# FFN down projections as seven block products per K pair instead of eight, in four passes, with POOL forming the differences of weight blocks

## The chip, the cores and the metric

One NeuronCore of a Trainium2 chip runs the whole program. The metric is the device time in microseconds (us) of one execution; the median of three timed executions of the kernel before is 2356.09 us. Engines: PE is TensorE's matmul stream and PEld its weight loads, DVE is VectorE, ACT is ScalarE, POOL is GpSimd, SP is SyncE, which issues the loads here.

## What is computed

Two decoder layers on a residual stream of 512 tokens by 1024 features, all float32. Each layer has two SwiGLU feed-forward blocks (FFN), a token mixer and a cross-attention. Only the FFN is touched by the change, and in it the last product:

```
def swiglu(x, w_gate, w_up, w_down):
    return (jax.nn.silu(x @ w_gate) * (x @ w_up)) @ w_down

h += 0.5 * rms_norm_post(swiglu(rms_norm_pre(h), w_gate, w_up, w_down))   # four times in all
```

w_gate and w_up are 1024 x 2816, w_down is 2816 x 1024. The 2816 hidden features are 22 blocks of 128, taken two at a time: 11 pairs ("groups" in gate_up, "quads" in the changed down stage).

## The kernel before, in words

**Split operands.** Every large product is made of three matmuls: each operand is written as hi + lo, both of type fp32r, and `three` (lines 1680 to 1684) issues hi x lo, lo x hi and hi x hi into the same PSUM bank. A matmul here has 128 x 128 stationary and 512 moving columns (256 in a few places).

**Pieces of weights.** Weights come as pieces of 128 x 1024 float32. SP loads a piece into one of four slots of `raw` (`load`, L428). ACT writes its hi part to `whi` (`split`, L642 with a gain for gate_up, L638 without one), DVE subtracts and writes the lo part to `wlo` (L1074, L1069), and PE uses both. `whi` and `wlo` have four slots too. Splits run three pieces ahead of PE (LOOKAHEAD = 3): ACT may overwrite a slot when `pieces_used` says that PE is done with the piece four before, and SP may reload a raw slot when `lo_made` says that its lo part exists. Each engine takes its instructions strictly in the order in which the program was written, so a split, an eviction and a sum that stand in DVE's queue are done in that order whatever is ready.

**Stages.** A list of stages (`stages`) sets the order. An FFN before is gate_up of 6 groups, down, gate_up of 5 groups, down. A gate_up group is 4 pieces of 24 matmuls (256 gate and 256 up columns, features in the partitions). Behind it DVE scales the two results out of PSUM into `gate` and `up` (L1385, L1388), ACT applies Silu (L869), POOL multiplies (L592), ACT writes `mid_hi` (L871) and DVE `mid_lo` (L1391), two blocks of 128 features by 512 tokens. A down stage has two groups, one for each half of 512 output columns; a piece is two K blocks by 512 columns, and `token_major` runs for each K block and each of four token tiles the three matmuls, so a K block costs 24 matmuls in all. A group uses four PSUM banks, the next one the other four; DVE releases them after reading (`release_banks`).

**Result.** The first pass of an FFN is copied to `y_rows` (L1456), the second is added (L1133). `close_sublayer` then takes squares for the norm (ACT L669, `square_result`), the variance (DVE L1137), a power on POOL (`power`, L543), the gain (DVE L1144) and the update of `h` (DVE L1179, `update`). `last_group` on PE orders the last group by token tile and puts transposes of updated tiles of `h` (`updated_units`, L1764) among its matmuls, so that the next stage can open: `open_hi` (ACT L654) and `open_lo` (DVE L1102) make `xhi` and `xlo` from them, and `first_group` starts with half of the tokens.

POOL also makes constant tables once, in the first down stage (`make_tables`, L531 to L577), which even_in uses.

Of the kernel before, what the change touches and what calls it, by code (L numbers as in the profile page):

```python
# [35 lines left out]
D = 1024  # L36
SEQ = 512
MEM = 256
FF = 2816
# [18 lines left out]
FF_PASSES = ((0, 6), (6, 5))  # L58
# [7 lines left out]

def stages():
# [3 lines left out]
    def ffn(l, j):  # L71
        for n, (g0, ng) in enumerate(FF_PASSES):
            out.append(("gate_up", l, (j, n), ng, KT // PK))
            out.append(("down", l, (j, n), 2, ng))
# [26 lines left out]
def build(nc, A, out):  # L101
# [65 lines left out]
    rows = place("rows", [P, 3, P], f32, at(3072))  # L167
    lam_in = place("lam_in", [P, 4, 64], f32, at(3456))
# [6 lines left out]
    mid_hi = place("mid_hi", [P, 12, SEQ], f32r, at(0))  # L175
    mid_lo = place("mid_lo", [P, 12, SEQ], f32r, at(6144))
    gate = place("gate", [P, 2, SEQ], f32, at(12288))
    up = place("up", [P, 2, SEQ], f32, at(13312))
# [47 lines left out]
    def sem(name):  # L226
# [25 lines left out]
    gate_scaled, up_scaled, gate_silu, product_ready, mid_hi_ready, mid_lo_ready = map(sem, (  # L252
        "gate_scaled", "up_scaled", "gate_silu", "product_ready", "mid_hi_ready", "mid_lo_ready"))
# [50 lines left out]
    def straight_groups(ng):  # L304

        return 2 if ng % 2 == 0 else 1

# [11 lines left out]
    def ends_sublayer(kind, arg):  # L319
        return kind in ("mix_out", "xo") or (kind == "down" and arg[1] == 1)  # L320
# [18 lines left out]
    def columns(g):  # L339
        return slice(g * GC, (g + 1) * GC)  # L340

# [60 lines left out]
    def _(sp):  # L402
# [18 lines left out]
        def load(base, g, halves):  # L421


            slot = base % RAW_SLOTS
            if not isinstance(base, int) or base >= RAW_SLOTS or not isinstance(g, int) or g:
                sp.wait_ge(lo_made, base + 1 + 4 * g)
            for dst, src in halves(slot):
                sp.dma_start(dst, src).then_inc(raw_full[slot], 16)  # L428

# [33 lines left out]
        piece = ended = 0  # L463
        for kind, l, arg, ng, np_ in STAGES:
            first_piece = piece
            if kind == "gate_up":
                j, n = arg
                first = straight_groups(ng)
                g0 = FF_PASSES[n][0]
                for g in range(first):  # L470
                    for kp in range(4):
                        if piece + 4 * g + kp == 0:
                            load_x(0)
                        if piece + 4 * g + kp == 1:
                            load_x(1)
                        if piece + 4 * g + kp == RAW_SLOTS:
                            load_rest()
                        load(piece + 4 * g + kp, 0, gate_and_up(l, j, kp, (g0 + g) * 256))
                with sp.Fori(0, (ng - first) // 2) as i:
                    for q in range(2):  # L480
                        for kp in range(4):
                            load(piece + 4 * (first + q) + kp, 2 * i,
                                 gate_and_up(l, j, kp, (g0 + first + q) * 256 + i * 512))
                piece += 4 * ng
                continue
            for g in range(ng):
                for n_piece in range(group_pieces(kind, g, np_, arg)):
# [4 lines left out]
                    elif kind == "down":  # L492
                        j, n = arg
                        src = two_rows(A["ffn_w_down"][l, j], 2 * FF_PASSES[n][0] + 2 * kp, g * GC)
# [12 lines left out]
                    load(piece, 0, src)  # L507
# [18 lines left out]
    def _(pool):  # L526
# [52 lines left out]
        products = 0  # L579
        for kind, l, arg, ng, np_ in STAGES:  # L580
# [6 lines left out]
            if kind == "gate_up":  # L587
                def multiply(n):

                    pool.wait_ge(gate_silu, n)  # L590
                    pool.wait_ge(up_scaled, n)
                    g.tensor_tensor(up[:], gate[:], up[:], MUL).then_inc(product_ready, 1)  # L592
                first = straight_groups(ng)
                for q in range(first):
                    multiply(products + q + 1)
                with pool.Fori(0, (ng - first) // 2) as i:
                    for q in range(2):
                        multiply(products + first + q + 1 + 2 * i)
                products += ng
            elif kind == "down" and (l, arg) == (0, (0, 0)):  # L600
                make_tables()
            elif kind == "even_in":
# [24 lines left out]
    def _(act):  # L627
# [3 lines left out]
        def split(n):  # L631

            slot = n % RAW_SLOTS
            act.wait_ge(raw_full[slot], 32 * (n // RAW_SLOTS + 1))
            act.wait_ge(pieces_used, n + 1)
            gains = piece_gain[n]
            if gains is None:
                a(flat(whi[:, slot]), flat(raw[:, slot]), ACT.Copy).then_inc(hi_made, 1)  # L638
                return
            hi, full = piece_rows(whi, slot, len(gains)), piece_rows(raw, slot, len(gains))  # L640
            for k, c in enumerate(gains):
                last = a(hi[:, k, :], full[:, k, :], ACT.Copy, scale=vec[:, c:c + 1])  # L642
            last.then_inc(hi_made, 1)
# [16 lines left out]
        def square_result(kind, bank, t, g):  # L660

            src = PS[:, bank + t, :]
            if kind == "down":
                E.await_(y_ready)
                src = y_rows[:, t, columns(g)]
# [6 lines left out]
        def square_tile(kind, bank, t, done):  # L672
# [3 lines left out]
            elif kind != "down":  # L676
                E.await_(tile_done)
            square_result(kind, bank, t, 1)

        def close_sublayer(kind, n, n_stage):  # L680
# [4 lines left out]
            if kind != "down":  # L685
                act.wait_ge(pieces_used, done)
# [5 lines left out]
            if kind == "down":  # L692
                E.seen[tile_done.name] += TT - 1

            def next_h(t):
# [1597 lines left out]
```

## Time and profile before

| | |
|---|---|
| three timed runs | 2354.50, 2356.09, 2356.28 us; median 2356.09 us |
| the profiled execution | 2354.63 us, of which the span from first to last instruction is 2352.9 us |
| granted clock of TensorE, mean | 0.997 of full |
| PE busy | 2331.8 us, 99% of the span, 12035 matmuls |
| PEld busy | 1976.7 us, 84% |
| DVE busy | 1151.1 us, 49%, 1531 instructions |
| ACT busy | 881.6 us, 37%, 1442 instructions |
| POOL busy | 179.0 us, 8%, 150 instructions |
| DMA | 217.48 MB, mean 92 GB/s |

Busy time counts the time in which at least one instruction of the engine is in flight. Matmuls overlap: each is shown for 0.39 us, but a new one starts more often than that, so what a matmul costs in a dense stretch is read from starts and not from durations. Timeline rows give the start in us from the start of the span, then the duration, then engine, line and operation; in square brackets stands how long the engine sat idle before, and what ended that.

### The profile page before, as it was taken

The numbers are of one execution on the slowest core, as the hardware profiler recorded it, in microseconds if no ns is written. First come the engines' busy times: TensorE is split into PE (matmuls) and PEld (weight loads), VectorE is DVE, ScalarE is ACT, GpSimd is POOL, SyncE is SP. The second block draws the span as 40 slices with busy tenths as digits, with TensorE's granted clock in tenths as the row PEclk, the third lists the DMA queues.
The fourth block names the chain that finished last, engine by engine and source line by source line (L and its number), as shares of the span: only waits on it lengthen the run. The fifth ranks groups of instructions, "written<-read, shape, count | busy, mean of one in ns | idle before, by whom it ended". The sixth has DMA issues, their size and how long they took to land.

```text
span 2352.9 us, 30267 instructions
## 1 busy us (share of the span) xinstructions
PE 2331.8 (99%) x12035; PEld 1976.7 (84%) x12035; DVE 1151.1 (49%) x1531; ACT 881.6 (37%) x1442; POOL 179.0 (8%) x150
## 2 busy tenths in 40 slices
PE   8999999999999999999999999999999999999998
PEld 7888888888888888888888888888878888888887
DVE  4433436595645444433454433455996544443434
ACT  4322324444444443323333322335265443322322
POOL 0131100000000001100101000000000000100000
PEclk9999999999999999999999999999999999999999
DMA  5233332311222123233223332322322212332231
GB/s 183 81 108 98 92 114 76 104 63 58 79 83 97 63 72 111 86 107 99 94 95 99 98 99 90 107 90 90 108 72 84 88 54 90 99 108 94 85 107 72
DMA packets 170483, 217.48 MB, mean 92 GB/s; under 512 B 12952, under 2 KB 120824, under 8 KB 170360
## 3 DMA queue, kind: packets, MB, share of 16 engines
q1 hardware_dynamic: 170248, 215.75, 28.8%
q8 instruction: 84, 1.38, 0.2%
q14 instruction: 39, 0.32, 0.0%
q10 hardware_dynamic: 112, 0.03, 0.0%
HBM read 213.63 MB, written 2.10 MB: 92 GB/s over the span
## 4 chain that ended last, share of the span: by engine, by line
PE 98%; DVE 1%; ACT 1%; issue 0%; DMA 0%; ACTq 0%; POOLq 0%; POOL 0%; DVEq 0%
PE ps L1682 29%; PE ps L1683 29%; PE ps L1684 29%; PE ps L2120 1%; PE ps L2233 1%; PE ps L1764 1%; PE ps L2050 1%; PE ps L1866 1%; PE ps L2158 1%; PE ps L2064 0%; PE ps L1734 0%; PE ps L2209 0%; PE ps L2147 0%; PE ps L1718 0%; PE ps L2160 0%
## 5 line engine op out<-in xcount | busy, mean ns | idle before, releaser
L1682 PE MATMUL ps<-xlo,whi 128*128 128x512 f32 (+1 forms) x2032 | 752.1, 370 | 1.7 <-DVE wlo L1074 1.7
L1683 PE MATMUL ps<-xhi,wlo 128*128 128x512 f32 (+1 forms) x2032 | 748.9, 369 | 0.0
L1684 PE MATMUL ps<-xhi,whi 128*128 128x512 f32 (+1 forms) x2032 | 748.8, 368 | 0.0
L1074 DVE SCALAR_TENSOR_TENSOR wlo<-raw,vec,whi 128x512 fp32r<-128x512 f32 (+1 forms) x488 | 338.6, 741 | 412.4 <-ACT whi L642 411.1
L642 ACT ACTIVATE whi<-raw,vec 128x512 fp32r<-128x512 f32 (+1 forms) x488 | 318.6, 708 | 486.2 <-PE ps L1684 450.9
L1682 PEld LDWEIGHTS ps<-xlo,whi 128*128 128x128 f32 x2032 | 384.0, 189 | 65.7 <-issue 2.1
L1684 PEld LDWEIGHTS ps<-xhi,whi 128*128 128x128 f32 x2032 | 383.7, 189 | 63.9
L1683 PEld LDWEIGHTS ps<-xhi,wlo 128*128 128x128 f32 x2032 | 383.9, 189 | 63.1
L1069 DVE TENSOR_TENSOR wlo<-raw,whi 128x1024 fp32r<-128x1024 f32 x152 | 185.5, 1227 | 286.2 <-ACT whi L638 284.7
L638 ACT ACTIVATE whi<-raw 128x1024 fp32r<-128x1024 f32 x152 | 159.4, 1056 | 336.3 <-PE ps L1684 335.8
L1682 PE MATMUL ps<-wlo,mid_hi 128*128 128x512 f32 x704 | 274.4, 390 | 0.0
L1684 PE MATMUL ps<-whi,mid_hi 128*128 128x512 f32 x704 | 274.0, 389 | 0.0
L1683 PE MATMUL ps<-whi,mid_lo 128*128 128x512 f32 x704 | 273.9, 389 | 0.0
L592 POOL TENSOR_TENSOR up<-gate,up 128x1024 f32<-128x1024 f32 x44 | 105.2, 2391 | 1069.7 <-DVE up L1388 1069.7
L1684 PEld LDWEIGHTS ps<-whi,mid_hi 128*128 128x128 f32 x704 | 132.2, 188 | 27.5
L1683 PEld LDWEIGHTS ps<-whi,mid_lo 128*128 128x128 f32 x704 | 132.2, 188 | 27.2
L1682 PEld LDWEIGHTS ps<-wlo,mid_hi 128*128 128x128 f32 x704 | 132.2, 188 | 27.1
L1682 PE MATMUL ps<-wlo,xhi 128*128 128x512 f32 x352 | 138.7, 394 | 2.5 <-issue 2.5
L1684 PE MATMUL ps<-whi,xhi 128*128 128x512 f32 x352 | 137.2, 390 | 0.0
L1683 PE MATMUL ps<-whi,xlo 128*128 128x512 f32 x352 | 137.0, 389 | 0.0
L1391 DVE TENSOR_TENSOR mid_lo<-up,mid_hi 128x1024 fp32r<-128x1024 f32 x44 | 54.8, 1244 | 161.5 <-ACT mid_hi L871 161.5
L869 ACT ACTIVATE gate<-gate 128x1024 f32<-128x1024 f32 x44 | 46.7, 1061 | 223.6 <-DVE gate L1385 223.6
(248 smaller groups left out, 2213.4 us busy)
## 6 DMA issues: line engine op xcount, KB each, us to landing
raw<-ffn_w_gate_dram SPq DMA_DIRECT2D x176, 256.0 KB, 2.8
raw<-ffn_w_up_dram SPq DMA_DIRECT2D x176, 256.0 KB, 3.0
raw<-ffn_w_down_dram SPq DMA_DIRECT2D x176, 256.0 KB, 3.1
raw<-xattn_w_kv_dram SPq DMA_DIRECT2D x64, 256.0 KB, 3.0
raw<-even_w_in_dram SPq DMA_DIRECT2D x56, 256.0 KB, 2.9
raw<-odd_w_in_dram SPq DMA_DIRECT2D x42, 256.0 KB, 2.8
raw<-xattn_w_q_dram SPq DMA_DIRECT2D x32, 256.0 KB, 3.0
raw<-xattn_w_o_dram SPq DMA_DIRECT2D x32, 256.0 KB, 3.0
```

The lines of the kernel that those rows point to most:

```text
L592: g.tensor_tensor(up[:], gate[:], up[:], MUL).then_inc(product_ready, 1)
L638: a(flat(whi[:, slot]), flat(raw[:, slot]), ACT.Copy).then_inc(hi_made, 1)
L642: last = a(hi[:, k, :], full[:, k, :], ACT.Copy, scale=vec[:, c:c + 1])
L869: a(gate[:], gate[:], ACT.Silu).then_inc(gate_silu, 1)
L1069: v.tensor_tensor(flat(wlo[:, slot]), flat(raw[:, slot]), flat(whi[:, slot]).bitcast(f32), SUB).then_inc(lo_made, 1)
L1074: last = v.scalar_tensor_tensor(out=lo[:, k, :], in0=full[:, k, :], scalar=vec[:, c:c + 1], in1=hi[:, k, :].bitcast(f32), op0=MUL, op1=SUB)
L1391: v.tensor_tensor(mid_lo[:, 2 * g:2 * g + 2, :], up[:], mid_hi[:, 2 * g:2 * g + 2, :].bitcast(f32), SUB).then_inc(mid_lo_ready, 1)
L1682: mm(out_ap, lh, rl, start=start, stop=False, skip_group_check=skip_group_check)
L1683: mm(out_ap, ll, rh, start=False, stop=False, skip_group_check=skip_group_check)
L1684: return mm(out_ap, lh, rh, start=False, stop=stop, skip_group_check=skip_group_check)
L1764: last = T(x_unit(bank, t, b)[:, k, :], h[:, t, (4 * b + k) * P:(4 * b + k + 1) * P], ident[:])
L1866: last = nc.tensor.transpose(blocks_of(4, 6)[:, n, :], probs[:, i % 2, m, kt * P:(kt + 1) * P], ident[:])
```

## The change

The 22 K blocks of w_down are paired. For one pair ("quad" q) the tokens are cut into two halves of 256, the output columns into two halves of 512, and the 2 x 2 by 2 x 2 block product is formed with seven products: A11 B11 (P1), A12 B21 (P2), S4 B22 (P3), A22 T4 (P4), S1 T1 (P5), S2 T2 (P6), S3 T3 (P7). A are blocks of the hidden activations and S sums of them, B are blocks of the weight and T differences: T1 = B12 - B11, T2 = B22 - T1, T3 = T2 - B11, T4 = B21 - T2. A product of one quad is two token tiles of three 128x512 matmuls.

* **Passes.** An FFN has four passes with gate_up groups 3, 2, 3, 3 and down quads 2, 3, 3, 3. A down stage has one list of units (one unit is one 128x512 block of B or T), two to a piece: first the units of B21, B11 and T1 of all quads but the last, then those of the last quad, then T2, B22, T3, T4.
* **PE.** `down` runs P2, P1, P5 of the early quads, then of the last one, then P6, P3, P7, P4, token tile by token tile. P1 and P6 and P7 and P4 share two banks: P6 accumulates on P1 after DVE has read P1, and so on, so PE waits for `product_read` before P6, P3, P7 and for each tile of P4.
* **DVE.** Before: one read per tile and group of columns in two passes (32 copies, 32 adds). After: in each pass P1, P2, P5, P6 are read two tiles at a time (128x1024) and P3, P7, P4 tile by tile. The reads stand in the queue between the splits. `gate` and `up` become halves of one tile `mid`; the wait ahead of the gate eviction is for the whole chain of the group before. Four sums of 128x256 (S1 to S4) follow POOL's product. `mid_lo` is made in two instructions (three and four blocks of 256 tokens), with splits between them in the last group of a stage.
* **ACT.** Splits of units (128x512); `mid_hi` in two instructions, likewise with splits between them.
* **POOL.** T1 ahead of the last product of a gate_up stage. In the down stage: T2 as one instruction per raw slot (128x1024, and 128x512 where there are three quads), then T3 and T4 (each 128 x 512 nq elements). `make_tables` moves to even_in.
* **SP.** B11, B12 and B21 are loaded to tiles of their own (`load_corners`, 3 nq loads of 256 KB) behind the first gate_up group's loads; B22 goes through the raw slots. The hardware loops over gate_up groups are written out.

The core of the diff (PE's and DVE's placement, POOL's work):

```diff
-FF_PASSES = ((0, 6), (6, 5))
+FF_GROUPS = ((0, 3), (3, 2), (5, 3), (8, 3))
+FF_QUADS = ((0, 2), (2, 3), (5, 3), (8, 3))
+def down_units(nq):
+    early, late = range(nq - 1), nq - 1
+    out = [("B21", q) for q in early] + [("B11", q) for q in early] + [("T1", q) for q in early]
+    out += [("B11", late), ("B21", late), ("T1", late)]
+    return out + [(name, q) for name in ("T2", "B22", "T3", "T4") for q in range(nq)]
```

POOL, in gate_up:

```diff
+                for g_ in range(ng):
+                    if g_ == ng - 1:
+                        pool.wait_ge(w11_loaded, 16 * (quads + nq))
+                        pool.wait_ge(w12_loaded, 16 * (quads + nq))
+                        difference(k, w12, flat(w12[:, 0:nq, :]), flat(w11[:, 0:nq, :]))
+                    products += 1
+                    pool.wait_ge(gate_silu, products)
+                    pool.wait_ge(up_scaled, products)
+                    g.tensor_tensor(mid[:, 4:8, :], mid[:, 4:8, :], mid[:, 0:4, :], MUL).then_inc(product_ready, 1)
```

POOL, in a down stage:

```diff
+                pool.wait_ge(lo_made, t1_piece + 1 + RAW_SLOTS)
+                for i in range(0, nq, 2):
+                    n = min(2, nq - i)
+                    ins = g.tensor_tensor(w12[:, i:i + n, :], raw[:, (first_raw + i // 2) % RAW_SLOTS, 0:n, :],
+                                          w12[:, i:i + n, :], SUB)
...
+                E.own()
+                pool.wait_ge(combined, 4 * k + 2)
+                difference(k, w11, flat(w12[:, 0:nq, :]), flat(w11[:, 0:nq, :]))
+                pool.wait_ge(w21_loaded, 16 * (quads + nq))
+                difference(k, w21, flat(w21[:, 0:nq, :]), flat(w12[:, 0:nq, :]))
```

ACT, in gate_up:

```diff
                     act.wait_ge(gate_scaled, mids)
-                    a(gate[:], gate[:], ACT.Silu).then_inc(gate_silu, 1)
+                    a(mid[:, 4:8, :], mid[:, 4:8, :], ACT.Silu).then_inc(gate_silu, 1)
+                    if g == ng - 1:
+                        split_next()
                     act.wait_ge(product_ready, mids)
-                    a(mid_hi[:, 2 * g:2 * g + 2, :], up[:], ACT.Copy).then_inc(mid_hi_ready, 1)
+                    a(mid_hi[:, slot, 4:7, :], mid[:, 4:7, :], ACT.Copy).then_inc(mid_hi_ready, 1)
+                    if g == ng - 1:
+                        split_next()
+                    act.wait_ge(sums_ready, mids)
+                    a(mid_hi[:, slot, 0:4, :], mid[:, 0:4, :], ACT.Copy).then_inc(mid_hi_ready, 1)
```

DVE, in gate_up behind the evictions of gate and up:

```diff
+                    if g == ng - 1:
+                        split_next()
+                    dve.wait_ge(product_ready, mids)
+                    a12, a22, a11, a21 = [mid[:, 4 + n, :] for n in range(4)]
+                    E.run(v.tensor_tensor(mid[:, S1, :], a21, a22, ADD))
...
+                    dve.wait_ge(mid_hi_ready, 2 * mids - 1)
+                    v.tensor_tensor(mid_lo[:, slot, 4:7, :], ...).then_inc(mid_lo_ready, 1)
+                    if g == ng - 1:
+                        split_next()
+                    dve.wait_ge(mid_hi_ready, 2 * mids)
+                    v.tensor_tensor(mid_lo[:, slot, 0:4, :], ...).then_inc(mid_lo_ready, 1)
```

DVE, in a down stage:

```diff
+            at_piece = {2: ("P1", "P2", "P5"), 3: ("P6",), 4: ("P3a", "P3b"), 5: ("P7a", "P7b"), 6: ("P4a", "P4b")} if nq == 2 else \
+                {3: ("P1", "P2"), 4: ("P5",), 6: ("P6",), 7: ("P3a", "P3b"), 8: ("P7a",), 9: ("P7b",), 10: ("P4a", "P4b")}
+            for n in range(2, len(down_pieces(nq))):
+                split_next()
+                for name in at_piece.get(n, ()):
+                    read[name]()
```

DVE, in the last pass of an FFN (`close_down`):

```diff
+            open_lo(0, x_banks[0])
+            split_next()
+            read["P4a"]()
+            made = weigh(2, 0)
+            open_lo(1, x_banks[1])
+            split_next()
+            read["P4b"]()
```

PE, in a down stage behind P1, P2 and P5:

```diff
+            pe.wait_ge(product_read, r0 + 1)
+            for t in range(2):
+                one_tile(u0, t, S2, x)
+            pe.wait_ge(product_read, r0 + 3)
+            for t in range(2):
+                one_tile(u0 + nq, t, S4, z)
+            pe.wait_ge(product_read, r0 + 4)
+            for t in range(2):
+                one_tile(u0 + 2 * nq, t, S3, x)
+            E.group += 2
+            if opens:
+                wait_banks(E.group)
+                updated_units(0)
+            pe.wait_ge(product_read, r0 + 7)
+            one_tile(u0 + 3 * nq, 0, A22, x, range(1))
+            if opens:
+                updated_units(1)
+            one_tile(u0 + 3 * nq, 0, A22, x, range(1, nq))
+            pe.wait_ge(product_read, r0 + 8)
+            one_tile(u0 + 3 * nq, 1, A22, x)
```

## Rows read from the trace of the kernel before

**Rows 1.** The page: span, busy time, and the chain that ended last.
```profile
span 2352.9 us, 30267 instructions
...
PE 2331.8 (99%) x12035; PEld 1976.7 (84%) x12035; DVE 1151.1 (49%) x1531; ACT 881.6 (37%) x1442; POOL 179.0 (8%) x150
...
PE 98%; DVE 1%; ACT 1%; issue 0%; DMA 0%; ACTq 0%; POOLq 0%; POOL 0%; DVEq 0%
```
**Rows 2.** Groups by form on PE: count, busy us, mean ns of one.
```profile
L1682 PE MATMUL ps<-wlo,mid_hi 128*128 128x512 f32 x704 | 274.4, 390 | 0.0
```
**Rows 3.** Timeline of DVE: the same instruction behind two successive gate_up groups.
```profile
281.71 1.22 DVE L1385 TENSOR_TENSOR gate<-ps,rsb 128x1024 f32<-128x1024 f32 x1 [2.59 <-PE ps L1684]
...
303.47 1.22 DVE L1385 TENSOR_TENSOR gate<-ps,rsb 128x1024 f32<-128x1024 f32 x1 [2.59 <-PE ps L1684]
```
**Rows 4.** Timelines around the start of the first down stage.
```profile
150.95 0.39 PE L1682 MATMUL ps<-wlo,mid_hi 128*128 128x512 f32 x1
...
151.15 1.23 DVE L1385 TENSOR_TENSOR gate<-ps,rsb 128x1024 f32<-128x1024 f32 x1 [3.06 <-PE ps L1684]
...
153.65 2.39 POOL L592 TENSOR_TENSOR up<-gate,up 128x1024 f32<-128x1024 f32 x1 [19.37 <-DVE up L1388]
...
156.08 1.06 ACT L871 ACTIVATE mid_hi<-up 128x1024 fp32r<-128x1024 f32 x1 [2.60 <-POOL up L592]
```
**Rows 5.** Groups by form on DVE, ACT and POOL: count, busy us, mean ns.
```profile
L1095 DVE TENSOR_TENSOR xlo<-y,xhi 128x512 fp32r<-128x512 f32 x28 | 18.4, 688 | 18.2 <-ACT xhi L734 18.2
...
L734 ACT ACTIVATE xhi<-y 128x512 fp32r<-128x512 f32 x28 | 16.5, 623 | 12.5 <-DVE y L1611 12.3
...
L592 POOL TENSOR_TENSOR up<-gate,up 128x1024 f32<-128x1024 f32 x44 | 105.2, 2391 | 1069.7 <-DVE up L1388 1069.7
```
**Rows 6.** Timeline of DVE: four successive 128x512 instructions.
```profile
352.43 2.48 DVE L1133 TENSOR_TENSOR y_rows<-ps,y_rows 128x512 f32<-128x512 f32 x4 [3.06 <-PE ps L1684]
```
**Rows 7.** Timeline: POOL and DVE at once, in the first down stage.
```profile
157.08 1.09 POOL L533 TENSOR_SCALAR_AFFINE_SELECT head_sel_f<-head_sel_f 8x1024 f32<-8x1024 f32 x1
157.17 2.07 DVE L1391 TENSOR_TENSOR mid_lo<-up,mid_hi 128x1024 fp32r<-128x1024 f32 x1 [3.66 <-ACT mid_hi L871]
...
168.62 1.23 DVE L1069 TENSOR_TENSOR wlo<-raw,whi 128x1024 fp32r<-128x1024 f32 x1 [4.13 <-ACT whi L638]
168.69 1.30 POOL L575 CAST level_mask<-level_f 128x128 int8<-128x128 f32 x1
...
171.79 0.29 POOL L575 CAST level_mask<-level_f 128x128 int8<-128x128 f32 x1
```
**Rows 8.** Single lines of code: duration ns min/median/max, first and last start.
```profile
L616 POOL TENSOR_TENSOR ring<-ring,conv x2: 1277/1744/2212, 1783.1 to 1786.3; 128x512 f32<-128x512 f32 x2
L616 POOL TENSOR_TENSOR ring<-conv x1: 1441/1441/1441, 1723.3 to 1723.3; 128x512 f32<-128x512 f32 x1
...
L1326 DVE TENSOR_SCALAR conv<-u,vec x4: 540/542/1495, 1646.4 to 1723.5; 128x512 f32<-128x512 f32 x4
```
**Rows 9.** Timeline of PE: 256-column matmuls at the start of the kernel.
```profile
12.42 0.55 PE L1682 MATMUL ps<-xlo,whi 128*128 128x256 f32 x1 [1.74 <-DVE wlo L1074]
...
16.19 0.41 PE L1684 MATMUL ps<-xhi,whi 128*128 128x256 f32 x1
16.40 0.31 PE L1682 MATMUL ps<-xlo,whi 128*128 128x256 f32 x1
...
16.67 0.28 PE L1684 MATMUL ps<-xhi,whi 128*128 128x256 f32 x1
16.79 0.28 PE L1682 MATMUL ps<-xlo,whi 128*128 128x256 f32 x1
```
**Rows 10.** One stretch: busy us (instructions) by engine, granted clock, DMA.
```profile
590.00:592.00 2.00, 2.00 (x10) 2.00 (x11) 0.14 (x2) 0.66 (x1) 0.00 (x0) 0.50 0.00 0
```
**Rows 11.** Timelines around the end of the first FFN: last results of tiles 2, 3.
```profile
383.79 0.93 POOL L543 TENSOR_TENSOR rstd<-var,neg_half 128x1 f32<-128x1 f32 x1 [1.95 <-DVE var L1137]
...
385.56 1.28 DVE L1179 SCALAR_TENSOR_TENSOR h<-y_rows,rstd,h 128x1024 f32<-128x1024 f32 x1
```

More of the change, by code:

```diff
@@ L64, with down_pieces, piece_of @@
 N_VEC = CONV_TAPS + CONV_W * CONV_T
+def down_units(nq):
[3 more added lines that the diff above has]
+    return out + [(name, q) for name in ("T2", "B22", "T3", "T4") for q in range(nq)]
+def down_pieces(nq):
+    units = down_units(nq)
+    corners, sums = units[:3 * nq], units[3 * nq:]
+    return [part[n:n + 2] for part in (corners, sums) for n in range(0, len(part), 2)]
+def piece_of(nq, unit):
+    return unit // 2 if unit < 3 * nq else (3 * nq + 1) // 2 + (unit - 3 * nq) // 2
 def stages():
@@ L461, in forget_rows @@
             return halves
-        piece = ended = 0
+        piece = ended = loads = 0
         for kind, l, arg, ng, np_ in STAGES:
@@ L506, in _ @@
                         src = two_rows(w, 2 * kp, g * GC)
-                    load(piece, 0, src)
+                    load(loads, src)
+                    loads += 1
                     piece += 1
@@ L579, in _, with difference @@
         products = 0
+        def difference(k, out, a_, b_):
+            nq = downs[k][3]
+            E.run(g.tensor_tensor(flat(out[:, 0:nq, :]), a_, b_, SUB), combined)
         for kind, l, arg, ng, np_ in STAGES:
@@ L691, in close_sublayer @@
             E.group += 2
-            if kind == "down":
-                E.seen[tile_done.name] += TT - 1
-            def next_h(t):
-                E.await_(h_ready)
-                act.wait_ge(h_squared, E.made[h_squared.name])
-                square_h(t, h_scratch[:])
-            if not opens(n_stage):
-                for t in range(TT):
-                    square_tile(kind, second, t, done + n)
-                return
             square_tile(kind, second, 0, done + n)
@@ new lines, in close_down, with gained, weigh, release @@
+        def close_down(k, n_stage):
+            read = reads_of(k, False)
+            def gained(t, g):
+                quarter = y_rows[:, t, columns(g)]
+                E.run(v.tensor_tensor(quarter, quarter, post_gain[:, columns(g)], MUL),
+                      post_gain_used if (t, g) == (TT - 1, 0) else None)
+                return E.last
+            def weigh(t, g):
+                result_variance("down", t)
+                return gained(t, g)
+            def release():
+                E.release_banks()
+                E.group += 1
+            split_next()
+            split_next()
+            read["P1"]()
+            read["P2"]()
+            split_next()
+            read["P5"]()
+            split_next()
+            read["P6"]()
+            dve.wait_ge(post_gain_loaded, 16 * (ended[0] + 1))
+            ended[0] += 1
+            for t in range(2):
+                E.await_(y_squared)
+                gained(t, 0)
+            split_next()
+            read["P3a"]()
+            made = weigh(0, 1)
+            read["P3b"]()
+            release()
+            split_next()
+            update(0, made)
+            read["P7a"]()
+            made = weigh(1, 1)
+            update(1, made)
+            read["P7b"]()
+            for t in (2, 3):
+                E.await_(y_squared)
+                gained(t, 1)
+            if not opens(n_stage):
+                read["P4a"]()
+                made = weigh(2, 0)
+                update(2, made)
+                read["P4b"]()
+                release()
+                made = weigh(3, 0)
+                update(3, made, 2)
+                return
+            x_banks = [x_bank(t, E.group + 1) for t in range(TT)]
+            open_lo(0, x_banks[0])
+            split_next()
+            read["P4a"]()
+            made = weigh(2, 0)
+            open_lo(1, x_banks[1])
+            split_next()
+            read["P4b"]()
+            release()
+            update(2, made)
+            made = weigh(3, 0)
+            split_next()
+            update(3, made)
+            split(E.piece + LOOKAHEAD)
+            open_lo(2, x_banks[2])
+            input_variance()
+            open_lo(3, x_banks[3])
+            split_rstd()
```

524 lines of the change are left out of this document (351 added, 173 removed).

## The prediction

> **What bounds the kernel now.** I read the page first: PE is busy for 2331.8 of the 2352.9 us, the chain that ended last is 98% PE, and DVE has half of the span free [rows 1]. So time goes only where PE does less, and comes wherever PE has to wait. A matmul's 390 ns [rows 2] overlaps the next one's; its cost is the distance of starts: the gate eviction stands at 281.71 and at 303.47 us, 21.76 us apart with 96 matmuls between, 0.2267 us each [rows 3]. The down products begin in the same rhythm and show no wait. Then I read what stands between a gate_up group's last matmul and its finished hidden blocks [rows 4], because the down stage now feeds on it at once, and the prices of DVE, ACT and POOL [rows 5, 6]. Last, how POOL and DVE behave at the same time [rows 7, 8], because POOL gets long instructions beside DVE's splits.
>
> **What goes.** Each of 704 steps of three matmuls [rows 2] stands for one K block, token tile and column half. Seven products for eight leave 616, so 264 matmuls go: 264 x 0.2267 = 59.8 us, all on PE, 15.0 us for each of four FFNs. The number of gate_up matmuls, the bytes loaded and the 256 KB size of a load stay.
>
> **What a down stage asks of the other engines.** A unit (one quad's block) costs PE six matmuls, 1.36 us. It costs DVE one 128x512 subtraction: 0.69 us alone [rows 5], 0.61 us in a row (2.48 us for four, [rows 6]); ACT's copy is 0.62 us. A stage of three quads is 21 units, 28.6 us of PE. In that time DVE has about 27 us: two evictions 2.4, ten or so units of the next pieces and T1_2 about 10, four sums 1.6, mid_lo 2.1, fourteen tile reads 8.3, first splits of the next stage 4. By the sum DVE would just keep up. It is the order that fails.
>
> **The walk of a three-quad stage**, from its first matmul (150.95 in the row, t = 0). Gate eviction 0.2, product on POOL 2.7 to 5.1, mid_hi from 5.1 [rows 4]. T1 of the last quad is split behind the four sums (done at about 7.8; one is 0.41 us, as 1024 elements take 1.23 [rows 4] and 512 take 0.69 [rows 5], 0.54 us per 512) and the first mid_lo (8.7): 9.4. PE has its first nine units done at 9 x 1.36 = 12.2, and waits 0.3 us among them for mid_lo. Now it needs DVE's read of P1. That read stands in DVE's queue behind the splits of T2_0, T2_1, T2_2 and B22_0, and T2 can be split only after POOL has made it. POOL takes 2.39 us for 1024 elements [rows 5] and 1.28 for 512 [rows 8], so 2.18 ns an element and 3.50 us for 1536. T2 is two instructions, 3.67 us.
> If POOL and DVE didn't hinder each other: T2 would be ready at 13.1, ACT's two copies of it at 14.3, DVE's splits would end at about 15.9 and P1's read at 17.1. PE, ready at 12.6, waits 4.5 us.
>
> **They do hinder each other.** A mid_lo of 1.23 us takes 2.07 us when it starts 0.09 us into a POOL instruction of 1.09 us; a POOL cast of 0.29 us takes 1.30 us when it starts just behind a split of 1.23 us [rows 7]. For the very instruction in question: POOL's 512-element addition takes 1.28 us and once 2.21 us, and a DVE tensor_scalar of 0.54 us takes 1.50 us where it starts at 1723.5, beside the POOL tensor_tensor that started at 1723.3 [rows 8]. So one waits nearly for the end of the other: 1723.5 + 1.50 - 0.54 = 1724.5, 0.2 to 0.3 us before POOL's end at 1723.3 + 1.44. Splits, sums, mid_lo, gains and updates have both inputs in SBUF; the reads of PSUM have one and don't suffer.
> The Trainium skill, "SBUF — State Buffer", section "Who interferes with whom", says that a DVE instruction with two SBUF inputs contends with a GpSimd instruction that reads SBUF, and that the one that comes first has the shared pair for the whole instruction. By that rule the walk is the one below, by the opposite it is the 4.5 us above; the rows side with the rule.
>
> With it: the split of the next piece waits for the product (until 4.8), mid_lo's second part holds POOL's T2 back to 10.4, T2 ends at 14.0. POOL goes straight on with T3, 3.50 us. DVE gets in at 17.2 for one split; T4 was asked for meanwhile and takes the next 3.5 us, to 21.3. Then three splits, 1.8 us, and P1's read, 1.2: 24.0. PE has waited since 12.6: **11.4 us**. After that PE and DVE run level, with 0.5 and 0.4 us lost before the two tiles of P4, where P7's reads stand behind splits. Sum for a three-quad pass: 0.3 + 11.4 + 0.9 = 12.6 us.
> The order "T4 after one split" is a choice between bounds: if DVE's splits all go before T4, P1 is read at 20.8 and PE waits 8.2 us. No row shows who wins after a back-to-back row of such DVE instructions against a long POOL one; I take turns, as POOL asked first.
>
> **The two-quad pass** (the first of each FFN). PE has six units, 8.2 us, plus 1.3 us in which it waits for the banks that gate and up are just read from (2.6 us against the 1.4 us of the one unit ahead). ACT's and DVE's queues have T2's split ahead of mid_hi and of the sums. POOL: product to 5.0, T2 7.4, T3 9.8; one split of DVE 10.2; T4 12.3; the other split, sums, mid_lo, four more splits and the second mid_lo are 7.8 us; P1's read 20.1. PE waits 10.7 us, and 1.0 us before P4: 13.0 us in all.
>
> **The closing pass.** Before, its matmuls and the next stage's ran on without a wait, though each tile has a square, a power on POOL (0.93) and an update of h (1.28) behind it [rows 5, 11]. After it, tile 0's transposes wait 1.4 us and tile 1's 1.1 us for updates that stand behind a read each. xlo of tile 1 stands behind the split, P4a's read, its square on ACT, the variance and a gain, 3.4 us even with an idle DVE, against P4b's 2.0 us on PE; with DVE's backlog of about 4 us I take 5.6 us, and 0.3 us for tile 2. Sum 8.4 us (bounds 1.4 and 12), with 11.7 us of the pass before it: 20.1.
>
> **Half rate.** At the start of the kernel, after idle time, 256-column matmuls start 0.21 us apart until 16.40 and 0.12 us apart from there, 4.0 us from 12.42 [rows 9]; and behind one-column matmuls the granted clock is 0.50 [rows 10]. These are 1.2 and 2.4 GHz. An idle time of 11 us should bring it back: 4.0 us at half rate cost 4.0 x (1 - 0.12/0.21) = 1.7 us. Sixteen long waits: 28 us (bounds 0, and 56 if it lasts twice as long).
>
> **Costed at nothing.** Corner loads, six or nine of 256 KB in a burst: SP issues them behind the group's first four loads, and a group is 21.8 us long. POOL's T1, 3.5 us, lies in the last group's 21.8 us. Longer gate_up chain (sums, two mid_lo): about 5 us more of DVE in a group where half is free. make_tables: even_in needs it some 90 us later. Code written out instead of loops.
>
> **Sum.** 2354.6 (profiled execution; the median is 1.5 above) - 59.8 + 4 x (13.0 + 12.6 + 12.6 + 20.1) - 8.4 (the last FFN opens nothing) + 28 = **2547.6**, against the median 2549.
>
> **Rivals.**
> *DVE and POOL don't block each other here*: pass 0 waits 7.7 (T2 7.4, its copies and splits 9.3, the same 7.8 us of queue: 17.1) + 1.3 + 1.0 = 10.0 us, the others 4.5 + 0.9, the close 8.4: 4 x (10.0 + 5.4 + 5.4 + 12.9) - 8.4 = 126 us of waits, less 59.8, plus 28 at half rate: 2449. For it: only a few overlaps are shown; against it: each shown one blocks. 15%.
> *DVE keeps POOL out*: three of four passes wait 8.2 and not 11.4, 39 us less: 2510. 18%.
> *The waits are hidden*: T2 comes while PE is on P1, P2 and P5. It decides at one point: P1 must be read within 12.2 us of the stage's start (8.2 with two quads). Then only the 59.8 us count, and a few us for the close: 2300. For it: DVE is half idle and 15 us of PE per FFN are sure. Against it: POOL's product and T2 alone take 2.4 + 3.7 us behind an eviction that ends at 2.6, and four splits and the read 4: 12.7 even without a sum or a mid_lo. 7%.
> *Reads and splits pile up further*, so that the next gate_up starts late too (2 us a pass) or half rate lasts twice as long: above 2585. 8%.
> The change does what it says in arithmetic: nothing in the diff lets a product be skipped.
>
> **The numbers.** Forecast 52%, rivals 15, 18, 7 and 8%. Range 2430 to 2590: down to the rival without blocking and 20 us for the close's bounds, up by half a doubled half-rate cost. Faster by over 0.2% (about what a measurement of this kernel can tell from no change) is the hidden case alone, 7%; within 0.2% 1%; slower 92%.
>
> **What would show it.** Right: 616 steps of three down matmuls, not 704; PE idle some 10 us before the first S2 matmul of each of 16 stages, ended by DVE's read of P1; POOL instructions of 3.5 us back to back; splits of T2 with durations of 3 to 4 us, not 0.69; DVE's busy time up by these blocked durations; clock 0.50 in the stretches behind the waits. Wrong: PE busy without gaps at P6, or a wait that ends on DMA (the corners), or on ACT.

## The result and the profile after

| | before | after |
|---|---|---|
| device time, median of 4 runs, us | 2355.57 | 2595.65 |
| profiled execution / its span, us | 2354.63 / 2352.9 | 2596.32 / 2594.6 |
| granted clock of TensorE, mean | 0.997 | 0.951 |
| PE waits longer than 8 us | 0 | 16 |

The ratio is 1.1019 (95% interval 1.1000 to 1.1038): 240 us slower, with 264 matmuls fewer. The forecast was 2549 us, its upper end 2590.

The page of the changed kernel, against [rows 1]: span, busy time, the chain that ended last.

```profile
span 2594.6 us, 30573 instructions
...
PE 2336.0 (90%) x11771; PEld 1956.9 (75%) x11771; DVE 1576.2 (61%) x2067; ACT 999.1 (39%) x1706; POOL 398.6 (15%) x226
...
PE 76%; DVE 13%; issue 4%; POOL 3%; ACT 3%; DMA 1%; SPq 0%; POOLq 0%; ACTq 0%; DVEq 0%
```

PE's share fell from 99% to 90%. DVE stands at 61% busy (time in which POOL holds it up counted in), and yet it is the engine that PE waits for. The view of waits, PE only (waiting line, awaited line: us in total, times, longest):

```profile
PE ps L2076 <- DVE y_rows L1347: 146.1, 26, 11.1
PE ps L2076 <- DVE y_rows L1343: 42.3, 4, 10.6
PE ps L1962 <- DVE rsb L1280: 17.5, 3, 6.1
PE ps L1962 <- DVE xlo L1292: 14.0, 3, 4.7
...
PE ps L2044 <- DVE h L1327: 6.8, 6, 1.2
PE ps L2076 <- DVEq L1651: 4.6, 4, 1.1
PE ps L2076 <- DVE mid_lo L1665: 3.8, 12, 0.3
```

L1347 and L1343 are DVE's reads of the products. Among the 26 waits of L1347 are 12 of 11.1 us, in the three-quad stages; the 4 of L1343, 10.6 us each, are those of the two-quad stages. All 16 stand before P6. L1292 and L1327 belong to the closing pass, L1651 to the banks of gate and up. The third row, 17.5 us at the opening of FFN 2, 3 and 4, is in no term of the prediction's sum.

The groups by form that answer to [rows 2, 5] (busy us, mean ns of one):

```profile
L2076 PE MATMUL ps<-wlo,mid_hi 128*128 128x512 f32 x616 | 261.5, 425 | 196.9 <-DVE y_rows L1347 146.1 <-DVE y_rows L1343 42.3 <-DVEq L1651 4.6
...
L1253 DVE TENSOR_TENSOR wlo<-w,whi 128x512 fp32r<-128x512 f32 x264 | 264.0, 1046 | 150.4 <-ACT whi L781 149.8
...
L1253 DVE TENSOR_TENSOR wlo<-raw,whi 128x512 fp32r<-128x512 f32 x44 | 28.7, 682 | 0.0
...
L1656 DVE TENSOR_TENSOR mid<-mid 128x256 f32<-128x256 f32 x44 | 66.6, 1515 | 72.0 <-POOL mid L694 72.0
...
L674 POOL TENSOR_TENSOR w<-w,w 128x1536 f32<-128x1536 f32 x36 | 129.2, 3605 | 1.7
```

616 steps of three matmuls, not 704. The same line L1253 on the same shape takes 682 ns on average where its source is the raw slot, and 1046 ns where it is a tile that POOL works on in the same stretch. The first sum (L1656, 128x256) takes 0.41 to 0.43 us in 28 of its 44 runs, as its three sisters do (below). In the other 16 it starts beside T1, which POOL begins right behind the product of the group before the last: 2.6 us beside a T1 of 2.4, 3.7 us beside one of 3.5, and so a mean of 1515 ns. No wait of PE follows from it.

**One stage in a timeline.** The second down stage, three quads, which starts at 163.35 us. Rows: start, duration, engine, line; in brackets the idle time before and what ended it.

```profile
163.35 0.39 PE L2076 MATMUL ps<-wlo,mid_hi 128*128 128x512 f32 x1
...
166.06 2.40 POOL L694 TENSOR_TENSOR mid<-mid 128x1024 f32<-128x1024 f32 x1 [15.90 <-DVE mid L1650]
...
166.95 2.66 DVE L1253 TENSOR_TENSOR wlo<-w,whi 128x512 fp32r<-128x512 f32 x2 [1.04 <-ACT whi L781]
169.53 0.41 DVE L1656 TENSOR_TENSOR mid<-mid 128x256 f32<-128x256 f32 x1
...
172.46 1.22 DVE L1670 TENSOR_TENSOR mid_lo<-mid,mid_hi 128x1024 fp32r<-128x1024 f32 x1
...
172.71 4.46 POOL L703 TENSOR_TENSOR w<-raw,w 128x1024 f32<-128x1024 f32 x2 [4.26 <-DVE wlo L1253]
177.31 3.44 POOL L674 TENSOR_TENSOR w<-w,w 128x1536 f32<-128x1536 f32 x1
...
178.38 7.34 DVE L1253 TENSOR_TENSOR wlo<-w,whi 128x512 fp32r<-128x512 f32 x3 [4.70 <-ACT whi L781]
...
180.70 3.87 POOL L674 TENSOR_TENSOR w<-w,w 128x1536 f32<-128x1536 f32 x1
...
181.22 4.50 DVE L1253 TENSOR_TENSOR wlo<-w,whi 128x512 fp32r<-128x512 f32 x2
...
186.25 2.54 DVE L1347 TENSOR_TENSOR y_rows<-ps,y_rows 128x1024 f32<-128x1024 f32 x2
...
187.51 0.79 PE L2076 MATMUL ps<-wlo,mid_hi 128*128 128x512 f32 x1 [11.06 <-DVE y_rows L1347]
```

(The row at 181.22 is the later two of the three splits at 178.38. The two 128x1536 rows of POOL, L674, are T3 and T4.) T2 ends at 177.17, 13.8 us into the stage; POOL goes on with T3. DVE's three splits, 0.6 us each when alone, take 7.34 us: the first ends only at 181.3, just behind T3's end at 180.75; the second waits for T4's end at 184.57. P1 is read by 187.4, 24.1 us into the stage.

**Half rate.** The stretches around that wait: length, busy us (instructions) of PE, PEld, DVE, ACT and POOL, then the granted clock, DMA share and GB/s.

```profile
160.00:176.00 16.00, 15.67 (x69) 12.53 (x68) 9.71 (x13) 4.53 (x6) 5.69 (x3) 1.00 0.00 0
176.00:188.00 12.00, 0.94 (x4) 0.52 (x3) 9.51 (x6) 3.23 (x6) 8.43 (x3) 0.61 0.00 0
188.00:204.00 16.00, 15.24 (x58) 12.05 (x58) 12.33 (x18) 6.13 (x10) 0.00 (x0) 0.87 0.41 134
```

And PE's timeline behind it:

```profile
188.53 0.63 PE L2081 MATMUL ps<-whi,mid_hi 128*128 128x512 f32 x1
188.96 0.63 PE L2076 MATMUL ps<-wlo,mid_hi 128*128 128x512 f32 x1
...
192.31 0.39 PE L2081 MATMUL ps<-whi,mid_hi 128*128 128x512 f32 x1
192.54 0.39 PE L2076 MATMUL ps<-wlo,mid_hi 128*128 128x512 f32 x1
```

Starts are 0.43 us apart until 192 and 0.23 us from there: 1.2 and then 2.4 GHz, with 4.5 us at the lower level behind the wait.

**Where the 242 us of span went.** I sorted the distances between successive matmul starts over the whole trace and took as excess what each has over the 0.2267 us of the dense rhythm (less for narrower matmuls), after against before:

* over 0.6 us, the waits: 252.5 against 8.6 us, so +243.9;
* 0.43 us, half rate: 38.1 against 3.8, so +34.3;
* 0.21 us, half rate with fewer columns: +5.2;
* 0.45 to 0.6 us: +7.6;
* 0.23 to 0.40 us: +7.3.

With -59.8 for the matmuls that makes 2352.9 + 238.5 = 2591.4, 3 us short of the span.

### The profile page after: what moved, and what is told of

Read it like the earlier page. It is cut to its first block, busy times and chain, and to the rows that moved or that the text cites. A ratio compares the mean times of both kernels' runs of the same rounds, so it can differ in the third digit from the quotient of the medians.

```text
span 2594.6 us, 30573 instructions
## 1 busy us (share of the span) xinstructions
PE 2336.0 (90%) x11771; PEld 1956.9 (75%) x11771; DVE 1576.2 (61%) x2067; ACT 999.1 (39%) x1706; POOL 398.6 (15%) x226
## 4 chain that ended last, share of the span: by engine, by line
PE 76%; DVE 13%; issue 4%; POOL 3%; ACT 3%; DMA 1%; SPq 0%; POOLq 0%; ACTq 0%; DVEq 0%
PE ps L1962 20%; PE ps L1964 20%; PE ps L1963 20%; DVE wlo L1253 6%; PE ps L2076 2%; POOL w L703 2%; PE ps L2080 2%; PE ps L2081 2%; DVE y_rows L1347 2%; ACT whi L781 1%; PE ps L2586 1%; PE ps L2473 1%; PE ps L2403 1%; PE ps L2044 1%; DVE wlo L1264 1%
## 5 line engine op out<-in xcount | busy, mean ns | idle before, releaser
L1962 PE MATMUL ps<-xlo,whi 128*128 128x512 f32 (+1 forms) x2032 | 756.6, 372 | 33.3 <-DVE rsb L1280 17.5
L2076 PE MATMUL ps<-wlo,mid_hi 128*128 128x512 f32 x616 | 261.5, 425 | 196.9 <-DVE y_rows L1347 146.1
L1253 DVE TENSOR_TENSOR wlo<-w,whi 128x512 fp32r<-128x512 f32 x264 | 264.0, 1046 | 150.4 <-ACT whi L781 149.8
L694 POOL TENSOR_TENSOR mid<-mid 128x1024 f32<-128x1024 f32 x44 | 105.4, 2396 | 1141.9 <-DVE mid L1650 1141.9
L2080 PE MATMUL ps<-whi,mid_lo 128*128 128x512 f32 x616 | 252.7, 410 | 0.0
L2081 PE MATMUL ps<-whi,mid_hi 128*128 128x512 f32 x616 | 251.3, 408 | 0.0
L781 ACT ACTIVATE whi<-w 128x512 fp32r<-128x512 f32 x264 | 149.6, 620 | 257.0 <-PE ps L2076 81.3
L674 POOL TENSOR_TENSOR w<-w,w 128x1536 f32<-128x1536 f32 (+1 forms) x48 | 159.4, 3337 | 2.3
L633 POOL TENSOR_TENSOR rstd<-var,neg_half 128x1 f32<-128x1 f32 (+3 forms) x39 | 34.0, 872 | 742.8 <-DVE var L1318 440.5
L2081 PEld LDWEIGHTS ps<-whi,mid_hi 128*128 128x128 f32 x616 | 123.5, 201 | 28.3
L1259 DVE TENSOR_TENSOR wlo<-raw,whi 128x1024 fp32r<-128x1024 f32 x64 | 78.0, 1223 | 101.2 <-ACT whi L758 101.0
```

The costliest lines, as they stand in the source:

```text
L674: E.run(g.tensor_tensor(flat(out[:, 0:nq, :]), a_, b_, SUB), combined)
L694: g.tensor_tensor(mid[:, 4:8, :], mid[:, 4:8, :], mid[:, 0:4, :], MUL).then_inc(product_ready, 1)
L781: last = a(whi[:, slot, i, :], unit_source(k, name, q), ACT.Copy)
L1253: last = v.tensor_tensor(wlo[:, slot, i, :], unit_source(k, name, q), whi[:, slot, i, :].bitcast(f32), SUB)
L1962: mm(out_ap, lh, rl, start=start, stop=False, skip_group_check=skip_group_check)
L2076: opening = mm(out, hi, wlo[:, slot, i, :], start=fresh, stop=False, skip_group_check=True)
```

## Experiments

The theory: each long wait is set by DVE's order and by the mutual exclusion of DVE and POOL. Rivals: queue order alone; exclusion alone; DVE has no time at all for what the scheme asks of it; and, for what the sum lacked, corner loads and half rate. Each version below is one execution, but for hoisted, which has four; differences are taken from the changed kernel's median, 2595.65 us, whose four executions lie within 3.3 us.

**no_t34: POOL's T3 and T4 cut to 8 elements.** T3 and T4 are otherwise left out of the computation; everything that waits for them still does.

```diff
-                difference(k, w11, flat(w12[:, 0:nq, :]), flat(w11[:, 0:nq, :]))
+                E.run(g.tensor_tensor(w11[:, 0, 0:8], w12[:, 0, 0:8], w11[:, 0, 0:8], SUB), combined)
...
-                difference(k, w21, flat(w21[:, 0:nq, :]), flat(w12[:, 0:nq, :]))
+                E.run(g.tensor_tensor(w21[:, 0, 0:8], w21[:, 0, 0:8], w12[:, 0, 0:8], SUB), combined)
```

> POOL makes T1 and T2 as before, but of T3 and T4 only 8 elements each; the splits then work on blocks without the differences. Theory A (DVE and POOL exclude each other, so T3 and T4 hold DVE's splits of T2 back by two instructions of 3.5 us less what one of DVE's instructions fits between): the long wait before P6 falls from 11.1 to about 5.8 us in the twelve three-quad stages and from 10.6 to about 7.3 us in the four two-quad ones, 77 us less in all, and splits of T2 last 0.6 to 0.7 us; about 2519 us. Rival B (the wait is DVE's order alone: reads behind splits that wait for T2 itself): nothing changes, 2596 us. Rival C (DVE simply has too much to do in a down stage): the wait goes elsewhere, over 2580 us.

Measured 2518.12 us, 77.5 less. Its waits of PE:

```profile
PE ps L2076 <- DVE y_rows L1347: 80.9, 26, 5.7
PE ps L2076 <- DVE y_rows L1343: 29.0, 4, 7.3
```

The longest wait falls from 11.1 to 5.7 us in the three-quad stages and from 10.6 to 7.3 in the two-quad ones, where 5.8 and 7.3 were expected. Half of the former is the time that T3 and T4 hold DVE back, though no one yet waits for T3 or T4 themselves. The other half is there without them.

**reads_early: P1 and P2 read ahead of the first splits of T2.**

```diff
-                {3: ("P1", "P2"), 4: ("P5",), 6: ("P6",), ...
+                {4: ("P5",), 6: ("P6",), ...
+            for name in first_reads:
+                read[name]()
             for n in range(2, len(down_pieces(nq))):
                 split_next()
```

> DVE reads P1 and P2 ahead of the splits of T2, not behind four of them; nothing is left out. Theory A: PE then waits for the first two T2 units' lo parts and no longer for the read of P1: three-quad stages 11.1 to about 9.0 us, two-quad ones 10.6 to about 9.5 us, 30 us less in all: about 2566 us, and the releaser of the wait is the split of T2. Rival B (order of the queue is what the wait is made of): the waits fall by the whole length of four splits and a read, to 4 us or less, under 2490 us.

Measured 2565.31 us, 30.3 less. Its waits of PE:

```profile
PE ps L2079 <- issue: 105.5, 12, 8.8
PE ps L2079 <- DVE y_rows L1343: 37.5, 4, 9.4
```

The 12 waits of the three-quad stages are 8.8 us, and they no longer end at a read. The view names no releaser ("issue"), but in the second down stage the split of the second T2 unit ends at 185.25 us and PE starts at 185.35: PE now waits for the splits of T2, which POOL's T3 and T4 hold up as before (2.91 and 3.90 us for two of them). Order alone is not it; taking away one of two late things shows the other.

**sp_order: the corner loads behind the last gate_up group's loads** where they would otherwise stand in an FFN's first group.

```diff
-                    if g == 0 and piece:
+                    if piece and g == (0 if n else ng - 1):
```

> In the first stage of the second, third and fourth FFN the corner loads are issued behind the last group's loads instead of the first group's. Theory: the wait that SP has ahead of them (until PE is through the first piece's second half) no longer holds back the loads of the second group, ACT's two waits of 19 us for a DMA go, and with them three waits of PE of 5.6 to 6.1 us and the half rate behind them: 18 to 24 us less, about 2575 us. Rival (the transfers themselves are late, by sheer bytes of the corners): the DMA waits stay, 2590 us or more.

Measured 2572.88 us, 22.8 less, and the row `rsb L1280` is gone from PE's waits. The cause in the changed kernel, view of the waits of SP's queue (`load_corners`, L498):

```profile
SPq L498 <- PE ps L1964: 122.2, 3, 44.3
```

and the opening of the second FFN's first stage in its timeline (L502 are the corner loads, `w` their tiles):

```profile
930.84 2.71 SPq L502 DMA_DIRECT2D w<-ffn_w_down_dram  x6
...
940.06 4.07 ACT L762 ACTIVATE whi<-raw,vec 128x512 fp32r<-128x512 f32 x6 [19.82 <-DMA raw<-ffn_w_up_dram]
...
942.76 0.68 DVE L1280 COPY rsb<-ps 128x512 f32<-128x512 f32 x1
...
943.55 0.77 PE L1962 MATMUL ps<-xlo,whi 128*128 128x512 f32 x1 [6.14 <-DVE rsb L1280]
```

SP stands at `pieces_used` until PE has used the first group's first piece, and the second group's weights queue behind that wait: ACT has nothing to split for 19.8 us, and DVE's copy of `rsb`, behind a split in its queue, comes 6 us late. The load that ACT waits for is late twice. SP issues it only at 934.08 us, behind the wait and the six corner loads (930.84 to 933.55); and behind their bytes it lands at 940.04, after 6.0 us where the median of such loads is 3.3. By an estimate from these figures some 5 us of PE's 6.1 would go without the six loads ahead, but only because the wait of 44 us had used up all the lead before. sp_order moves the wait and the loads together and does not part the two.

**warm: 42 matmuls of 128x128 by 512 columns into an unused bank** ahead of the wait for P1's read. They fill the wait and change no result.

```diff
+            for _ in range(42):
+                mm(PS[:, second, :], mid_hi[:, downs[k][2] % MID_SLOTS, A12, 0:P], xhi[:, 0, :], start=True, stop=True)
             pe.wait_ge(product_read, r0 + 1)
```

> PE is given 42 matmuls of 128x512 into an unused bank (9.5 us at 0.2267 us each) just before it waits for the read of P1; they add nothing to the result. Theory (half rate behind the long waits costs some 50 us over all): the granted clock stays up, the matmuls hide in the wait, and the kernel gains 30 to 45 us: about 2557 us, mean clock over 0.98. Rival (after the wait DVE sets the pace, so that PE's rate does not matter): the clock rises, the time stays within 10 us of 2596.

Measured 2567.48 us, 28.2 less, clock 0.988. The same stretch as above:

```profile
176.00:188.00 12.00, 10.28 (x46) 8.19 (x45) 11.89 (x9) 3.15 (x6) 6.29 (x2) 1.00 0.00 0
```

So the half rate behind the 16 long waits costs 28 us net. By starts, the 0.43 us distances cost 9.2 instead of 38.1 us and those of 0.45 to 0.6 us 6 us less, 35 us together. Some 6 of the other 7 are waits again: with the 152.3 us of the 672 added matmuls in them they come to 258.3 us where they were 252.5. Where PE goes on faster, it waits longer for DVE: 2.1 us more for `h`, 1.2 for `rsb`, about 2 before P6. The expectation, 2557 us, was 10 us too low, as it took nearly all slow spacings to hang on these waits. Against before, 20 us of them are left in this kernel: 5 us each of 0.43 and 0.21 us distances, 8 us of 0.23 to 0.40 and 1 us of 0.45 to 0.6.

**t3_later: POOL starts T3 when DVE has split all T2.**

```diff
                 E.own()
+                pool.wait_ge(lo_made, base_piece + piece_of(nq, down_units(nq).index(("T2", nq - 1))) + 1 + RAW_SLOTS)
                 pool.wait_ge(combined, 4 * k + 2)
```

> Only edit: POOL starts T3 when DVE's lo parts of all T2 units are written, not straight behind T2. Theory (DVE's order plus POOL and DVE excluding each other at T3): DVE gets its splits of T2 and the read of P1 before the 3.6 us instruction, so the waits before P6 in three-quad stages fall from 11.1 to about 6 us, with some 2 us new before P3 or P7, where T3 and T4 now come late; two-quad stages stay at 10.6 to 12 us. About 7 us less for each FFN plus some half rate: near 2565 us (2555 to 2580). Rival (T3 is only in the way of work that is late for other reasons; the wait is set by T2's own lateness): the time stays at 2590 to 2600 or rises, as T3 comes later.

Measured 2563.24 us, 32.4 less. An added wait on POOL makes the kernel faster. The same stage, timelines of DVE and POOL:

```profile
180.12 1.90 DVE L1254 TENSOR_TENSOR wlo<-w,whi 128x512 fp32r<-128x512 f32 x3 [4.70 <-ACT whi L782]
181.94 0.69 DVE L1254 TENSOR_TENSOR wlo<-raw,whi 128x512 fp32r<-128x512 f32 x1
182.54 2.55 DVE L1348 TENSOR_TENSOR y_rows<-ps,y_rows 128x1024 f32<-128x1024 f32 x2
185.00 5.67 DVE L1254 TENSOR_TENSOR wlo<-raw,whi 128x512 fp32r<-128x512 f32 x2
...
182.79 7.34 POOL L674 TENSOR_TENSOR w<-w,w 128x1536 f32<-128x1536 f32 x2 [3.88 <-DVE wlo L1254]
```

The same three splits take 1.90 us where they took 7.34. At 182.54 two reads of PSUM take 2.55 us beside POOL's T3, as they took 2.54 with POOL idle; the next two splits, with both inputs in SBUF, take 5.67 us. The two-quad stages (longest wait 11.5 us, where it was 10.6) got a little worse, as expected.

**dve_diff: DVE makes T2, T3 and T4 itself**, each just before the splits that need it; POOL keeps T1 and the product.

```diff
+            differences = {2: "T3", 3: "T4"} if nq == 2 else {2: "T2", 5: "T3", 6: "T4"}
             for n in range(2, len(down_pieces(nq))):
+                if n in differences:
+                    on_dve(k, differences[n])
                 split_next()
```

> Only edit: T2, T3 and T4 are made by DVE, each just before the splits that need it; POOL keeps T1 and the product. Order of the reads, order of the units and the corner loads are as in the changed kernel. DVE's work grows by some 5.5 us for a three-quad stage (1536 elements three times). Theory (half or more of the wait before P6 is POOL and DVE excluding each other, the rest is DVE's order): T2 is there at about 12, two splits end at 15, P1 is read at 16.5, so PE waits about 4 us and not 11.1, with 1 to 2 us new before P3, P7 or P4; closings stay; near 2465 us (2440 to 2500), although DVE does more. Rival (the exclusion is small; the long POOL instructions only fill time in which DVE would be late anyway): more work on DVE lengthens the waits, 2590 us or more.

Measured 2536.2 us, 59.5 less: DVE gets some 5.5 us more work for each three-quad stage, and PE waits less. Of its waits:

```profile
PE ps L2086 <- DVE y_rows L1348: 79.9, 36, 3.9
PE ps L2086 <- DVE y_rows L1344: 33.7, 4, 8.4
```

The wait before P6 came out as expected (4.3 us between starts in the three-quad stages, where 4 was expected). The total did not (2465): T3 stands ahead of other splits and reads and makes a new wait of 2 to 3 us later in the stage, and two-quad stages still wait 8.4 us, since P1's read there still stands behind T3 and two splits. So DVE's lack of time is not what held the changed kernel back: with more work on DVE the kernel is faster, where the rival had 2590 us or more. It becomes the next bound.

**hoisted: all of it at once.** T2, T3 and T4 of quads 0 and 1 on DVE in the last gate_up group, where it has time; of quad 2 in the down stage; reads as soon as the product is there; PE in the order P2, P5, P1; the two-quad stage waits for P1's read alone before P6; tile 1's `open_lo` ahead of P4's first read; and sp_order's edit.

```diff
+                    if g == ng - 1:
+                        differences(k_down, 0, 2)
...
+            order = "5 6 P6 7 P3a P3b release 8 P7a P7b 9 P4a P4b release" if nq == 2 else \
+                "T2 P1 5 P2 6 P5 T3 7 T4 8 P6 9 P3a P3b release 10 P7a 11 P7b 12 P4a 13 P4b release"
+            for what in order.split():
```

> POOL makes only T1 and the product. DVE makes T2, T3 and T4 itself, for quads 0 and 1 in the last gate_up group behind its last split (1024 elements each), for quad 2 in the down stage (512 each). PE takes the products in the order P2, P5, P1; DVE reads P1 as soon as it is there, ahead of splits; the two-quad stage waits only for P1's read before P6; the corner loads stand behind the last group's loads; in the closing stage tile 1's open_lo stands before P4's first read. Theory (the waits are queue order and exclusion, not a lack of engine time): the wait before P6 falls from 11 to 1 to 3 us, in the two-quad stage too; with closings of 4 to 7 us and little half rate this gives 2310 to 2365 us, about the kernel before or a little under it. Rival (DVE has no room: 27 us of work in 28.6 us of PE without the differences, and 2 to 4 us more with them): the waits move to P3, P7 and P4, some 5 us a stage, and the time stays at 2380 to 2440 us.

Measured 2398.34 us, 197 less than the changed kernel, ratio to the kernel before 1.0189 (1.0172 to 1.0206). The page and the waits of PE:

```profile
PE 2301.1 (96%) x11771; PEld 1928.0 (80%) x11771; DVE 1574.6 (66%) x2151; ACT 998.7 (42%) x1706; POOL 226.8 (9%) x166
```
```profile
PE ps L2067 <- DVE h L1333: 16.9, 9, 2.4
PE ps L2099 <- DVE y_rows L1349: 13.0, 8, 2.8
PE ps L2099 <- DVE mid_lo L1684: 12.9, 12, 1.1
PE ps L2099 <- DVE y_rows L1353: 8.2, 6, 2.9
PE ps L2099 <- DVE wlo L1240: 8.0, 12, 0.7
PE ps L1985 <- DVE xlo L1279: 7.6, 3, 2.5
```

The long waits are gone; what is left is short and spread over six causes. Between theory (2310 to 2365) and rival (2380 to 2440) the total falls to the rival. The place of the waits is only in part the rival's: 21 us of them end at a read of a product, 24 at `h` and `xlo` in the closings. The stretches around one three-quad stage fit a DVE without room:

```profile
140.00:175.00 35.00, 32.99 (x144) 26.36 (x143) 31.95 (x42) 15.67 (x25) 3.56 (x2) 1.00 0.06 17
175.00:185.00 10.00, 10.00 (x46) 8.29 (x45) 9.74 (x15) 4.14 (x7) 0.00 (x0) 1.00 0.63 203
```

DVE is busy for 41.7 of 45 us here. That this is the cause is argued from these figures; no version with less work on DVE was run. By starts, 82.8 us of distances over 0.6 us and 17 us of slower spacings stand against the 59.8 saved: 40 of the 43 us by which the kernel is slower than before. A three-quad stage loses about 3 us so, of the 4.1 it saves (three quads at 1.36 us); a closing one that opens the next stage 12 us, the two-quad one 5. No version was run that beats the kernel before, and none in which only the middle passes use the seven products; by an estimate from these figures it would gain some 1 us a pass.

## Why the prediction came out as it did

**Right, what goes:** 616 steps instead of 704, -59.8 us.

**Right, the walk of a three-quad stage.** Predicted: T2 ends at 14.0, P1 read at 24.0, wait 11.4 us. In the stage shown: 13.8, 24.1 and 11.06 us. Predicted 10.7 us for the two-quad stage, measured 10.6; 1.3 for the banks, measured 1.1; 8.4 for the closing, measured about 7 (4.7 for xlo, 2.3 for h). In all, without the openings, 243.9 - 17.5 = 226.4 us of waits against 224.8 in the sum. The rule that sided with the rows (the Trainium skill, "SBUF — State Buffer", section "Who interferes with whom") held: a split beside a POOL instruction waits for its end (7.34 us for three, 1.90 with POOL idle), and PSUM reads do not (2.55 us for two beside T3). Its counterpart, 4.5 us of wait without exclusion, can be held against the 4.3 us of dve_diff, where POOL makes none of the differences; the two are not the same kernel, since there DVE has to make T2 itself.

**Right, the choice between turns and DVE first.** The first split gets in between T3 and T4, and then POOL has its turn. The rival at 2510 us (8.2 us of wait) is refuted by 11.06; so are the one without blocking (2449) and the hidden one (2300). The fourth, "above 2585", has the measured time but not what happened: PE has no wait over 0.6 us at the opening of a gate_up stage inside an FFN, and half rate behind the sixteen long waits lasts 3.1 to 5.7 us and not 8.

**Right, half rate behind the sixteen waits:** 28 us, by warm 28.2 net (35 by the spacings alone).

**Wrong, "Costed at nothing. Corner loads ... SP issues them behind the group's first four loads, and a group is 21.8 us long."** The step set the loads against a group's length and did not look at the wait in front of them: `load_corners` waits for `pieces_used` of a piece that PE has yet to use, SP's later loads are queued behind it, and with the lead of 21.8 us gone the six loads are in the way too. By sp_order it costs 22.8 us (17.5 us of waits in three openings and the slow spacings behind). With it alone the forecast would have been 2572, inside the range.

**Mis-sized, "Half rate".** The sum had only the sixteen waits. Beyond what warm removed, the trace has 20 us of slower spacings: some 10 us at half rate behind closings and openings (sp_order took some 4 of them), and 8 us of steps 0.23 to 0.40 us apart, most of them in the down stages, which stay in hoisted too. What causes the last is open.

The sum with the openings' 17.5 us, these 20, and the other waits as measured (1.6 more) is 2587 with 28 us of half rate, 2594 with 35; the profiled execution took 2596.3. The mechanism of the long waits was right; the upper end failed because the corner loads, costed at nothing, brought no upper bound of their own into the range. Nor does 2590 follow from the term given for it: even a fully doubled half-rate cost adds only 28 us and gives 2577, and the other 13 us have no term.

**A slip in the prediction's sum of DVE's work:** its seven items for a three-quad stage come to 28.4 us and not 27, against 28.6 us of PE. "Would just keep up" was already without slack, which is what hoisted then ran into.

## What to carry to other kernels

Fewer matmuls are worth only what the other engines can follow, and before costing it look at their order and not their busy share: PE waited some 235 us for a DVE that was 39% idle. Find the one operation that PE needs next and walk its engine's queue backwards to it. Work given to POOL was not free for DVE here: while a POOL subtraction ran, DVE's splits stood still, and DVE doing three of the four differences itself was 59 us faster. And a load that has to wait for a buffer goes behind the loads that needn't: price the wait first, and the transfer by what lead the wait leaves.

## What the runs showed of the hardware

DVE and POOL take turns: with both asking, one DVE split was let in between two long POOL instructions (T3 ended at 180.75, the split at about 181.3), then the next POOL instruction, shown from 180.70, took 3.87 us where T3 had taken 3.44, and the next split ended only behind it. A POOL subtraction of 128x1536 elements took 3.44 us where nothing held it up; DVE's of the same shape took 1.75 us in dve_diff. The same turns show in t3_later: beside T3 and T4 two splits take 1.80 and 3.95 us. A wait on POOL, placed ahead of T3, saved 32 us by itself. In the stage shown, half rate stayed for 4.5 us of matmuls behind the wait, near the 4.0 us taken from the kernel's start [rows 9]; over the sixteen waits it was 3.1 to 5.7 us.
